# Fetching rounded weights and their remainders with casting and adding DMAs in a two-block transformer kernel

## The chip, the cores and the metric

The kernel runs on one core of a Trainium2 chip. The metric is the time of one execution on the device in microseconds (us), the median of several runs. Below, PE is TensorE, ACT is ScalarE, DVE is VectorE, POOL is GpSimd and SP is SyncE; SP only issues DMAs here. A stall is time in which PE has nothing to do.

## What is computed

Two transformer blocks follow one another on a sequence of 512 tokens with a model width of 1024, all in float32. Cut to the matrix products, which are nearly all of the work:

```python
h = rmsnorm(x, norm_mix_g);  z = h @ w_in                      # 1024 x 5888: q, k, v, gates
y_a, y_b = mixer_a(...) @ w_out_a, mixer_b(...) @ w_out_b      # 1024 x 1024, 256 x 1024
x = x + (gate_a * y_a + gate_b * y_b) @ w_out
x = x + square(relu(rmsnorm(x) @ w_ff1)) @ w_ff2               # hidden 4096
x = x + sigmoid(rmsnorm(x) @ w_ple_gate) * (p @ w_ple)         # 1024 x 1024, 256 x 1024
...
x = x + 0.5 * (silu(h @ ffn1_w1) * (h @ ffn1_w3)) @ ffn1_w2    # second block, hidden 2816
x = x + hybrid_mixer(rms_norm(x), w_in_2, ...)                 # 1024 x 3584
x = x + memory_attention(rms_norm(x), rms_norm(mem), ...)      # mem: 256 rows; w_kv 1024 x 2048
x = x + 0.5 * (silu(h @ ffn2_w1) * (h @ ffn2_w3)) @ ffn2_w2
return rms_norm(x, norm_out)
```

## The kernel before

Every product is made of three, since TensorE is fed rounded numbers (type float32r, "fp32r" in the rows): a number a is split into its rounded value a_h and the remainder a_l = a - a_h, and w x = w_h x_h + w_h x_l + w_l x_h. Activations are kept transposed, features on the 128 partitions and the 512 tokens beside them, as pairs of tiles `h_h` and `h_l`. The weights are used once each. They lie in HBM in the order of use, cut into **panels** of 128 rows by 1024 columns (512 KB): the 8 blocks of 128x128 that make 128 output features out of 1024 inputs. A panel is 8 x 3 matmuls of 512 columns. Some panels are short: those of `w_out_b` and `w_ple` have 2 blocks (128x256, 128 KB, 6 matmuls) and alternate with full ones, of `w_out_a` and of `w_ple_gate`. Those for the 256 rows of `mem` are full panels whose matmuls have 256 columns. Let i be the number of a panel.

A panel passes through three buffers, chosen by i mod 3. SP loads it into `raw` (`load_panel`, L2728 to L2733). ACT copies each half of it, 128x512, into `wh`, which rounds it (`prep` of `scalar`, which records its copy at L1749). DVE, or POOL for a few panels, subtracts: `wl` = `raw` - `wh` (`prep` of `vector`, L2114, and of `gpsimd`, L2681). PE takes `wh` and `wl` (`mm_k`, L1459). A `raw` buffer is free for the next load once its subtraction is done; `wh` and `wl` are free once PE has used the panel (the event `("used", i)`, a PE signal). Panels 0 and 1 come in three pieces each (`load_piece`, `piece`), so that PE can start early.

The order of each engine's instructions is fixed when the kernel is built. `put` appends a step to `plan` and gives it a time on each engine from the guesses in `LENGTHS`; ACT, DVE and POOL then run their steps in the order of these times, SP in the order of `plan`. Each engine runs strictly in its order and waits where it stands. In `run`, when PE starts panel i, the load of panel i + 3 and the preparation of panel i + 2 are planned:

```python
            if part == 0:
                put("load", p.i + 3)
                put("prep", p.i + 2, 0)
            began[0] = clock[PE] - .5
            if part == parts // 2:
                put("prep", p.i + 2, 1)
```

Beside this, ACT and DVE move results out of PSUM, split activations, do the norms and the softmax. POOL adds the squares for the norms (`norm_add`, L2689, tile `ssum`) and multiplies in the SwiGLU (`silu`, L2693). In the step `ple`, which follows each `w_ple_gate` panel, two norms are summed at once, so that POOL has two adds for each pair of panels. Early in the kernel SP also writes a table of position biases to HBM (`d_tab`), waits until it has landed, and reads it back in twelve DMAs (`spread_table`); the weight loads planned after it stand behind it in SP's queue.

Of the kernel before, what the change touches and what calls it, by code (L numbers as in the profile page):

```python
# [187 lines left out]
def panel_banks(p, *args):  # L188
# [42 lines left out]
    "row1": ((ACT, .6), (DVE, .7)), "piece": ((ACT, .4), (DVE, .45)), "prep": ((ACT, .61), (DVE, .7)), "square": ((ACT, .6),), "add": ((POOL, 1.4),), "mean": ((ACT, .6), (DVE, .7)),  # L231
# [37 lines left out]
class Panel:  # L269
    def __init__(self, i, off, spec, ops, use, n, first, blocks, low):  # L270
        self.i, self.off, self.spec, self.ops, self.use, self.n, self.first = i, off, spec, ops, use, n, first
        self.blocks, self.low, self.ncol = blocks, low, len(spec[3])
        self.width = spec[2] * self.ncol
        if i < 2:
            self.cuts = [slice(0, 256), slice(256, 512), slice(512, 1024)]
        else:
            self.cuts = [slice(o, min(o + 512, self.width)) for o in range(0, self.width, 512)]
        self.done, self.landed = ("used", i), ("raw", i)
# [5 lines left out]
def build(nc, d):  # L284
# [23 lines left out]
    raw_t = [at(f"raw{i}", [128, 1024], O_RAW + 4 * i) for i in range(3)]  # L308
    wh_t = [at(f"wh{i}", [128, 1024], O_W + 8 * i, F32R) for i in range(3)]
    wl_t = [at(f"wl{i}", [128, 1024], O_W + 8 * i + 4, F32R) for i in range(3)]  # L310
# [425 lines left out]
    put("load", 2)  # L736
    put("load_mats")
    put("load_table")
    for i in (3, 4):
        put("load", i)  # L740
# [6 lines left out]
    for k in range(KT):  # L747
        clock[PE] = max(clock[PE], placed["row1", k]) + 1.36
        put("mm1", k)
        if k == 3:  # L750
            put("prep", 2, 0)
    put("prep", 2, 1)
    put("prep", 3, 0)
    put("prep", 3, 1)
# [634 lines left out]
    def last_halves(w2, ks, acts):  # L1389
# [16 lines left out]
        for h in range(2):  # L1406
            for n, p in enumerate(ps):
# [4 lines left out]
                if not h:  # L1412
                    put("prep", p.i + 2, 0)
                    put("prep", p.i + 2, 1)
# [17 lines left out]
    landed = [Signal(f"landed{i}", 16) for i in range(3)]  # L1432
# [15 lines left out]
    def tensor(e, gate):  # L1448
# [30 lines left out]
        def mm_k(p, k, n=slice(0, 512), use=None, last=False):  # L1479
            t, c, use = p.ops[k], p.piece(k), use or p.use  # L1480
            out = use.ap[:, 0:n.stop - n.start]
            wh, wl = (w[p.i % 3][:, 128 * k:128 * k + 128] for w in (wh_t, wl_t))
# [11 lines left out]
        def mm_blocks(p, i):  # L1494
# [3 lines left out]
            for k in range(nk):  # L1498
                t, c, b = p.ops[p.spec[1][0] + k], p.piece(k), p.blocks[i]
                wh, wl = (w[p.i % 3][:, 256 * k:256 * k + 256] for w in (wh_t, wl_t))  # L1500
# [238 lines left out]
    def scalar(e, gate):  # L1739
# [32 lines left out]
        def prep(i, c):  # L1772
            if i >= len(panels) or c >= len(panels[i].cuts):
                return
            p = panels[i]
            gate.wait_ge(p.landed, ("used", i - 3) if i > 2 else None)
            copy(wh_t[i % 3][:, p.cuts[c]], raw_t[i % 3][:, p.cuts[c]]).then_inc(*rounded.mark(("hi", i, c)))
# [312 lines left out]
        steps = {"start": start, "piece": piece, "prep": prep, "row1": row1, "square": norm_square, "mat_r": round_mats,  # L2090
# [17 lines left out]
    def vector(e, gate):  # L2108
# [20 lines left out]

        def prep(i, c):  # L2130
            if i >= len(panels) or c >= len(panels[i].cuts) or panels[i].low != "vector":
                return
            cut = panels[i].cuts[c]
            gate.wait_ge(("hi", i, c))
            sub(wl_t[i % 3][:, cut], raw_t[i % 3][:, cut], wh_t[i % 3][:, cut]).then_inc(*rest_left.mark(("lo", i, c)))
# [516 lines left out]
        steps = {"start": start, "piece": piece, "prep": prep, "row1": row1, "add": norm_add, "mean": mean, "rms": rms,  # L2652
# [21 lines left out]
    def gpsimd(e, gate):  # L2674

        def prep(i, c):
            if i >= len(panels) or c >= len(panels[i].cuts) or panels[i].low != "gpsimd":
                return
            cut = panels[i].cuts[c]
            gate.wait_ge(("hi", i, c))  # L2680
            e.tensor_tensor(wl_t[i % 3][:, cut], raw_t[i % 3][:, cut], wh_t[i % 3][:, cut].bitcast(F32), ALU.subtract).then_inc(*rest_left_g.mark(("lo", i, c)))  # L2681
# [19 lines left out]
        steps = {"prep": prep, "add": norm_add, "silu": silu, "last_out": last_out}  # L2701
# [6 lines left out]
    def sync(e, gate):  # L2708
# [17 lines left out]

        def load_panel(i):
            if i >= len(panels):  # L2728
                return
            p = panels[i]  # L2730
# [46 lines left out]
        steps = {"start": start, "load_x": load_x, "load_piece": load_piece, "load": load_panel, "load_mats": load_mats,  # L2777
# [68 lines left out]
```

## Time and profile before

| | |
|---|---|
| median of 3 runs | 2086.63 us (2085.16 to 2087.03) |
| the profiled execution's own time | 2087.62 us |
| its span, first to last instruction | 2085.8 us |
| mean granted TensorE clock, share of full speed | 0.985 |
| PE busy | 2041.7 us, 98% |
| DVE, ACT, POOL busy | 1212.0, 907.2, 220.7 us |
| moved by DMA | 191.53 MB, mean 92 GB/s |

PE busy is near the span. The difference, 44.1 us, is the idle time of PE. The granted clock tells at which of its two levels, 2.4 GHz (1.0) and 1.2 GHz, PE ran; a mean between them is a mixture. Durations of single matmuls overlap, so the rate is read from the number of matmuls in a window.

### The profile page before, as it was taken

How to read it: one execution, taken by the hardware profiler on the slowest of the kernel's cores; microseconds unless marked ns; L12 is line 12 of the kernel's file. 1: busy time of each engine (PE TensorE's matmuls, PEld its weight loads, DVE VectorE, ACT ScalarE, POOL GpSimd, SP SyncE). 2: the span in 40 equal slices, each digit the busy share in tenths (PEclk: the TensorE clock that was granted, in tenths of full speed). 3: DMA queues.
4: the chain of work that ended last, by engine and by line, in shares of the span. 5: the costliest groups of instructions: out<-in, count | busy, mean ns of one | idle time of the engine just before them, and what ended most of it. 6: DMA issues, size and time to landing. Idle time of an engine off the chain costs nothing.

```text
span 2085.8 us, 24995 instructions
## 1 busy us (share of the span) xinstructions
PE 2041.7 (98%) x9832; PEld 1694.1 (81%) x9832; DVE 1212.0 (58%) x2027; ACT 907.2 (43%) x1749; POOL 220.7 (11%) x170
## 2 busy tenths in 40 slices
PE   8999999999999999999999999999899999999997
PEld 6788888888888888878888888877888788888886
DVE  5768876466444445775544455877776555453444
ACT  4455554345423233643322334766654443332324
POOL 1102220001000001221100011100001011110101
PEclk9999999999999999999999999999999999999998
DMA  4312111243333232323232323222332033333222
GB/s 142 122 62 65 58 61 46 84 155 111 97 96 101 92 101 77 105 81 111 91 101 92 101 90 102 72 86 93 105 112 86 19 109 101 96 97 101 91 91 71
DMA packets 61633, 191.53 MB, mean 92 GB/s; under 512 B 6792, under 2 KB 14472, under 8 KB 61516
## 3 DMA queue, kind: packets, MB, share of 16 engines
q1 hardware_dynamic: 61516, 189.93, 28.6%
q8 instruction: 78, 1.28, 0.2%
q14 instruction: 39, 0.32, 0.1%
HBM read 187.69 MB, written 2.21 MB: 91 GB/s over the span
## 4 chain that ended last, share of the span: by engine, by line
PE 89%; DVE 5%; ACT 3%; DMA 1%; issue 1%; SPq 1%; POOL 0%; DVEq 0%; ACTq 0%
PE bank L1459 88%; PE bank L1463 1%; DVE tmp L2111 1%; DVE wl L2114 1%; SPq L2714 0%; DVE ssum L2111 0%; DVE rsq L2118 0%; DMA d_tab<-tab_sb 0%; ACT rsq L1760 0%; DMA x_sb<-d_xT 0%; ACT rsq L1758 0%; ACT tmp L1752 0%; DMA raw<-d_wts 0%; ACT pa L1885 0%; DVE tmp L2120 0%
## 5 line engine op out<-in xcount | busy, mean ns | idle before, releaser
L1749 ACT ACTIVATE wh<-raw 128x512 fp32r<-128x512 f32 (+1 forms) x698 | 416.6, 611 | 843.0 <-PE bank L1459 815.6
L1459 PE MATMUL bank<-h_h,wh 128*128 128x512 f32 x1536 | 616.4, 401 | 7.3 <-ACT h_h L1749 3.9
L1459 PE MATMUL bank<-h_l,wh 128*128 128x512 f32 x1536 | 601.4, 392 | 1.4 <-DVE h_l L2139 1.4
L1459 PE MATMUL bank<-h_h,wl 128*128 128x512 f32 x1536 | 601.4, 392 | 0.6 <-POOL wl L2681 0.6
L2114 DVE TENSOR_TENSOR wl<-raw,wh 128x512 fp32r<-128x512 f32 (+1 forms) x642 | 485.9, 768 | 90.7 <-ACT wh L1749 82.8
L1459 PEld LDWEIGHTS bank<-h_h,wh 128*128 128x128 f32 x1536 | 290.6, 189 | 72.9 <-ACT wh L1749 5.1
L1459 PEld LDWEIGHTS bank<-h_l,wh 128*128 128x128 f32 x1536 | 290.6, 189 | 62.5 <-issue 3.1
L1459 PEld LDWEIGHTS bank<-h_h,wl 128*128 128x128 f32 x1536 | 289.9, 189 | 62.8 <-POOL wl L2681 1.1
L2111 DVE TENSOR_TENSOR tmp<-bank,rstd 128x512 f32<-128x512 f32 x98 | 70.4, 719 | 119.3 <-PE bank L1459 119.3
L2681 POOL TENSOR_TENSOR wl<-raw,wh 128x512 fp32r<-128x512 f32 x56 | 78.5, 1409 | 333.5 <-ACT wh L1749 333.5
L2111 DVE TENSOR_TENSOR x_sb<-x_sb,bank 128x512 f32<-128x512 f32 (+1 forms) x66 | 42.0, 646 | 122.2 <-PE bank L1459 121.8
L2693 POOL TENSOR_TENSOR tmp<-tmp,rstd 128x512 f32<-128x512 f32 x44 | 59.9, 1362 | 494.6 <-ACT tmp L1920 494.6
L2689 POOL TENSOR_TENSOR ssum<-tmp,tmp 128x512 f32<-128x512 f32 (+1 forms) x9 | 11.8, 1319 | 869.6 <-ACT tmp L1752 869.6
L2395 DVE SCALAR_TENSOR_TENSOR x_sb<-bank,x_sb 128x512 f32<-128x512 f32 x45 | 31.1, 692 | 123.0 <-PE bank L1459 123.0
L1459 PE MATMUL bank<-f1act_h,wh 128*128 128x512 f32 x256 | 99.6, 389 | 0.0
L1459 PE MATMUL bank<-f1act_l,wh 128*128 128x512 f32 x256 | 99.6, 389 | 0.0
L1459 PE MATMUL bank<-f1act_h,wl 128*128 128x512 f32 x256 | 99.6, 389 | 0.0
L2111 DVE TENSOR_TENSOR tmp<-tmp,bank 128x512 f32<-128x512 f32 x53 | 36.3, 685 | 86.5 <-PE bank L1459 83.6
L2689 POOL TENSOR_TENSOR ssum<-ssum,tmp 128x512 f32<-128x512 f32 (+1 forms) x51 | 65.9, 1297 | 146.8 <-ACT tmp L1752 146.6
L1459 PE MATMUL bank<-f3act_h,wh 128*128 128x512 f32 (+1 forms) x194 | 71.8, 370 | 0.0
L1459 PE MATMUL bank<-f3act_h,wl 128*128 128x512 f32 (+1 forms) x194 | 71.7, 369 | 0.0
L1459 PE MATMUL bank<-f3act_l,wh 128*128 128x512 f32 (+1 forms) x194 | 71.6, 369 | 0.0
(485 smaller groups left out, 3296.3 us busy)
## 6 DMA issues: line engine op xcount, KB each, us to landing
raw<-d_wts SPq DMA_DIRECT2D x316, 512.0 KB, 3.5
raw<-d_wts SPq DMA_DIRECT2D x20, 384.0 KB, 3.0
x_sb<-d_xT SPq DMA_DIRECT2D x16, 256.0 KB, 5.0
raw<-d_wts SPq DMA_DIRECT2D x24, 128.0 KB, 2.0
d_yT<-x_sb SPq DMA_DIRECT2D x4, 384.0 KB, 2.9
tab<-d_ali SPq DMA_DIRECT2D x4, 256.0 KB, 3.9
tab<-d_dec SPq DMA_DIRECT2D x4, 256.0 KB, 3.2
mraw<-d_memT SPq DMA_DIRECT2D x8, 128.0 KB, 2.5
```

Source lines behind the costliest of these rows:

```text
L1459: return e.matmul(out, lhsT, rhs, start=opens(use), stop=True, skip_group_check=True)
L1463: return e.transpose(out, in_, ident)
L1749: return e.activation(out, in_, FN.Copy, **kw)
L2111: return e.tensor_tensor(out, a, b, op)
L2114: return e.tensor_tensor(out, a, h.bitcast(F32), ALU.subtract)
L2395: ins = e.scalar_tensor_tensor(x[nb], p.use.ap[:, :], scale, x[nb], ALU.mult, ALU.add)
L2681: e.tensor_tensor(wl_t[i % 3][:, cut], raw_t[i % 3][:, cut], wh_t[i % 3][:, cut].bitcast(F32), ALU.subtract).then_inc(*rest_left_g.mark((" ...
L2689: e.tensor_tensor(s, first, t, ALU.add).then_inc(*summed.mark((norm.key, "sum", k), norm.ts[k].free, norm.ts[0].free if k == 1 else None))
L2693: e.tensor_tensor(t.ap[:, :], t.ap[:, :], norm.r.ap[:, :], ALU.mult).then_inc(*summed.mark(("silu_r", p.i)))
```

## The change

The weights no longer pass through `raw` (except panels 0 and 1, which are loaded as before). POOL issues for each panel a DMA from HBM straight into `wh`; its destination has the type float32r, so the transfer converts. ACT then writes `wl` = -`wh` in one instruction of 128x1024. POOL issues a second DMA which reads the same weights from HBM again and adds them to `wl` in SBUF: `wl` = -`wh` + weights. DVE's and POOL's subtractions are gone. The space of the `raw` buffers makes a fourth pair `wh`, `wl` (on the place of the two `raw` buffers of panels 0 and 1). Buffers go by i mod 4, and the load of panel i + 3, planned at the start of panel i, waits until PE has used panel i - 1. SP keeps only the other loads and the output.

```diff
             if part == 0:
                 put("load", p.i + 3)
-                put("prep", p.i + 2, 0)
-            began[0] = clock[PE] - .5
-            if part == parts // 2:
-                put("prep", p.i + 2, 1)
+                put("rest", p.i + 2)
...
     def scalar
-        def prep(i, c):
-            gate.wait_ge(p.landed, ("used", i - 3) if i > 2 else None)
-            copy(wh_t[i % 3][:, p.cuts[c]], raw_t[i % 3][:, p.cuts[c]]).then_inc(*rounded.mark(("hi", i, c)))
+        def rest(i):
+            if i < len(panels):
+                gate.wait_ge(("hi", i, 0))
+                copy(wl_t[i % 4][:, 0:panels[i].width], wh_t[i % 4][:, 0:panels[i].width].bitcast(F32), scale=-1.0).then_inc(*rounded.mark(("minus", i)))
...
     def gpsimd
-        def prep(i, c):
-            gate.wait_ge(("hi", i, c))
-            e.tensor_tensor(wl_t[i % 3][:, cut], raw_t[i % 3][:, cut], wh_t[i % 3][:, cut].bitcast(F32), ALU.subtract).then_inc(...)
+        def load_panel(i):
+            if i < len(panels):
+                p = panels[i]
+                gate.wait_ge(*[("used", i - 4)] if i > 3 else [("lo", n, 2) for n in range(2)] if i == 3 else [])
+                e.dma_start(wh_t[i % 4][:, 0:p.width], source(p)).then_inc(*landed[i % 4].mark(("hi", i, 0)))
+
+        def rest(i):
+            if i < len(panels):
+                p = panels[i]
+                gate.wait_ge(("minus", i))
+                e.dma_start(wl_t[i % 4][:, 0:p.width], source(p), accum_op=ALU.add).then_inc(*added[i % 4].mark(("lo", i, 0)))
...
     def sync
-        def load_panel(i):
-            if i > 2:
-                gate.wait_ge(("lo", i - 3, len(panels[i - 3].cuts) - 1))
-            e.dma_start(raw_t[i % 3][:, 0:p.width], source(p)).then_inc(*landed[i % 3].mark(p.landed))
```

The order of SP's queue around `spread_table`, before. `raw_49` to `raw_51` are the three `raw` buffers, `bias` the bias tiles:

```order
L2733 DMA raw_51<-d_wts 128x1024 [waits s_rest_left_g]
L2733 DMA raw_49<-d_wts 128x1024 [waits s_rest_left]
L2714 DMA d_tab<-tab_sb 32x1x893 [waits s_dve_computed]
L2714 DMA bias_85<-d_tab 128x1x256 [waits s_loaded_row]
L2714 DMA bias_85<-d_tab 128x1x256 x3
L2714 DMA bias_86<-d_tab 128x1x128 x4
L2714 DMA bias_87<-d_tab 128x1x128 x4
L2714 DMA sel_sb<-d_sel 128x1028
L2714 DMA rope_sb<-d_rope 128x1024
L2733 DMA raw_50<-d_wts 128x1024 [waits s_rest_left_g]
```

and in the changed kernel:

```order
L2707 DMA mats_sb<-d_mats 128x648
L2707 DMA relb_sb<-d_relb 32x12
L2707 DMA hot_sb<-d_hot 32x893
L2707 DMA mask_sb<-d_mask 4x893
L2707 DMA d_tab<-tab_sb 32x1x893 [waits s_dve_computed]
L2707 DMA bias_86<-d_tab 128x1x256 [waits s_loaded_row]
```

No weight load stands behind the bias table any more; the weight loads are on POOL. POOL's queue of the changed kernel in the pairs of `w_ple` (128x256) and `w_ple_gate` (128x1024), one pair and the start of the next; `wh_51` to `wh_54` are the four `wh` buffers and `wl_55` to `wl_58` the `wl` beside them, `ssum_71` and `ssum_72` the sums of the two norms:

```order
L2682 TENSOR_TENSOR ssum_72<-ssum_72,tmp_64 128x512 [waits s_pool_computed,s_act_computed]
L2682 TENSOR_TENSOR ssum_71<-ssum_71,tmp_60 128x512 [waits s_pool_computed,s_act_computed]
L2668 DMA wh_52<-d_wts 128x1024 [waits s_banked]
L2668 DMA wh_53<-d_wts 128x256 [waits s_banked]
L2674 DMA wl_55<-d_wts 128x256 [waits s_rounded]
L2674 DMA wl_56<-d_wts 128x1024 [waits s_rounded]
L2682 TENSOR_TENSOR ssum_72<-ssum_72,tmp_62 128x512 [waits s_pool_computed,s_act_computed]
```

Before, POOL's queue had only the adds here:

```order
L2689 TENSOR_TENSOR ssum_71<-ssum_71,tmp_62 128x512 [waits s_pool_computed,s_act_computed]
L2689 TENSOR_TENSOR ssum_70<-ssum_70,tmp_59 128x512 [waits s_pool_computed,s_act_computed]
L2689 TENSOR_TENSOR ssum_71<-ssum_71,tmp_61 128x512 [waits s_pool_computed,s_act_computed]
```

Now two adds, which wait for ACT's squares, stand ahead of two loads and two adding DMAs in each pair. In the pairs of `w_out_b` and `w_out_a` POOL has in both kernels no adds, and now these rows:

```order
L2668 DMA wh_54<-d_wts 128x1024 [waits s_banked]
L2674 DMA wl_57<-d_wts 128x256 [waits s_rounded]
L2668 DMA wh_51<-d_wts 128x256 [waits s_banked]
L2674 DMA wl_58<-d_wts 128x1024 [waits s_rounded]
L2668 DMA wh_52<-d_wts 128x1024 [waits s_banked]
```

The load of a panel waits for PE (`s_banked`), the adding DMA for ACT (`s_rounded`).

## Rows read from the trace of the kernel before

**Rows 1.** The page: busy time; PE's share of the chain that ended last.

```profile
PE 2041.7 (98%) x9832; PEld 1694.1 (81%) x9832; DVE 1212.0 (58%) x2027; ACT 907.2 (43%) x1749; POOL 220.7 (11%) x170
...
PE 89%; DVE 5%; ACT 3%; DMA 1%; issue 1%; SPq 1%; POOL 0%; DVEq 0%; ACTq 0%
```

**Rows 2.** The page: costliest groups, busy and mean ns of one, then idle before.

```profile
L1749 ACT ACTIVATE wh<-raw 128x512 fp32r<-128x512 f32 (+1 forms) x698 | 416.6, 611 | 843.0 <-PE bank L1459 815.6
L2114 DVE TENSOR_TENSOR wl<-raw,wh 128x512 fp32r<-128x512 f32 (+1 forms) x642 | 485.9, 768 | 90.7 <-ACT wh L1749 82.8
L2681 POOL TENSOR_TENSOR wl<-raw,wh 128x512 fp32r<-128x512 f32 x56 | 78.5, 1409 | 333.5 <-ACT wh L1749 333.5
L2693 POOL TENSOR_TENSOR tmp<-tmp,rstd 128x512 f32<-128x512 f32 x44 | 59.9, 1362 | 494.6 <-ACT tmp L1920 494.6
```

**Rows 3.** Windows: PE, PEld, DVE, ACT, POOL busy (count), PEclk, DMA share, GB/s.

```profile
10.00:20.00 10.00, 8.48 (x30) 6.55 (x30) 8.44 (x13) 8.76 (x17) 2.23 (x2) 0.83 0.88 316
55.00:75.00 20.00, 15.19 (x77) 11.39 (x76) 12.87 (x23) 9.77 (x26) 2.97 (x2) 0.83 0.47 170
560.00:800.00 240.00, 240.00 (x1060) 198.74 (x1059) 101.62 (x153) 76.16 (x128) 0.00 (x0) 1.00 0.31 97
885.00:915.00 30.00, 25.65 (x99) 19.80 (x98) 18.52 (x23) 14.55 (x24) 8.46 (x6) 0.89 0.23 70
1450.00:1480.00 30.00, 22.84 (x103) 18.66 (x102) 23.86 (x45) 18.28 (x40) 6.42 (x7) 0.77 0.22 72
1490.00:1530.00 40.00, 40.00 (x306) 38.70 (x306) 33.21 (x70) 26.95 (x59) 0.00 (x0) 1.00 0.47 148
1535.00:1550.00 15.00, 11.97 (x40) 9.11 (x39) 10.19 (x17) 7.09 (x13) 0.00 (x0) 0.77 0.30 105
```

**Rows 4.** Timeline, 37 to 67 us: start, duration, engine, line, [idle before <-releaser].

```profile
37.46 0.77 SPq L2714 DMA_DIRECT2D d_tab<-tab_sb  x1
43.70 7.30 SPq L2714 DMA_DIRECT2D bias<-d_tab  x12
...
52.02 14.11 SPq L2733 DMA_DIRECT2D raw<-d_wts  x5
57.62 0.63 ACT L1749 ACTIVATE wh<-raw 128x512 fp32r<-128x512 f32 x1 [16.02 <-DMA raw<-d_wts]
...
58.31 0.50 PE L1459 MATMUL bank<-h_h,wh 128*128 128x512 f32 x1 [1.55 <-ACT wh L1749]
59.67 0.50 PE L1459 MATMUL bank<-h_h,wl 128*128 128x512 f32 x1 [0.63 <-POOL wl L2681]
66.79 0.96 PE L1463 MATMUL bank<-mats_sb,tmp 128*128 128x128 f32 x4 [2.64 <-DVE tmp L2111]
```

**Rows 5.** The chain that ended last, 885 to 898 us: start, length, what.

```profile
885.19 3.88 DVE wl L2114 x3
...
892.54 3.25 DVE wl L2114 x2
```

**Rows 6.** The page: DMA issues, count, size, median us from issue to landing.

```profile
raw<-d_wts SPq DMA_DIRECT2D x316, 512.0 KB, 3.5
raw<-d_wts SPq DMA_DIRECT2D x20, 384.0 KB, 3.0
...
raw<-d_wts SPq DMA_DIRECT2D x24, 128.0 KB, 2.0
```

**Rows 7.** Timeline, PE at two short panels of `w_ple`; ACT and POOL between and behind.

```profile
841.50 0.39 PE L1459 MATMUL bank<-p_op_h,wh 128*128 128x512 f32 x1
848.30 0.39 PE L1459 MATMUL bank<-p_op_h,wh 128*128 128x512 f32 x1
...
848.56 0.42 ACT L1749 ACTIVATE wh<-raw 128x256 fp32r<-128x256 f32 x1 [1.09 <-PE bank L1459]
...
856.38 2.55 POOL L2689 TENSOR_TENSOR ssum<-tmp,tmp 128x512 f32<-128x512 f32 x2 [18.54 <-ACT tmp L1752]
```

**Rows 8.** The timeline, 17 to 22 us: POOL and DVE side by side.

```profile
17.77 3.95 POOL L2681 TENSOR_TENSOR wl<-raw,wh 128x512 fp32r<-128x512 f32 x2 [17.33 <-ACT wh L1749]
18.18 4.09 DVE L2111 TENSOR_TENSOR ssum<-ssum,tmp 128x512 f32<-128x512 f32 x3
22.80 0.68 DVE L2111 TENSOR_TENSOR ssum<-ssum,tmp 128x512 f32<-128x512 f32 x1
```

More of the change, by code:

```diff
@@ L230 @@
 LENGTHS = {
-    "row1": ((ACT, .6), (DVE, .7)), "piece": ((ACT, .4), (DVE, .45)), "prep": ((ACT, .61), (DVE, .7)), "square": ((ACT, .6),), "add": ((POOL, 1.4),), "mean": ((ACT, .6), (DVE, .7)),
+    "row1": ((ACT, .6), (DVE, .7)), "piece": ((ACT, .4), (DVE, .45)), "load": ((POOL, 1.),), "rest": ((ACT, 1.02), (POOL, 1.)), "square": ((ACT, .6),), "add": ((POOL, 1.4),), "mean": ((ACT, .6), (DVE, .7)),
     "mean_mm": ((PE, .45),), "rms": ((ACT, 1.9), (DVE, 1.4)), "rcol": ((DVE, 2.8),), "table": ((PE, .5), (DVE, 1.1)),
@@ L276, in __init__ @@
         else:
-            self.cuts = [slice(o, min(o + 512, self.width)) for o in range(0, self.width, 512)]
-        self.done, self.landed = ("used", i), ("raw", i)
+            self.cuts = [slice(0, self.width)]
+        self.done = ("used", i)
     def piece(self, k):
@@ L735, in build @@
     put("load_x", (4, 5, 6, 7))
-    put("load", 2)
     put("load_mats")
     put("load_table")
-    for i in (3, 4):
-        put("load", i)
+    put("load", 2)
     for k in range(KT):
@@ L750, in build @@
         if k == 3:
[L751 to L754, printed above, removed]
+            put("rest", 2)
+            put("load", 3)
+    put("rest", 3)
+    put("load", 4)
     for k in range(KT):
@@ L1412, in last_halves @@
                 if not h:
-                    put("prep", p.i + 2, 0)
-                    put("prep", p.i + 2, 1)
+                    put("rest", p.i + 2)
                 if h and not n:
@@ L1428, in build @@
         clock[PE] += .1
-    landed = [Signal(f"landed{i}", 16) for i in range(3)]
+    landed, added = ([Signal(f"{n}{i}", 16) for i in range(4)] for n in ("landed", "added"))
     pieces = [[Signal(f"piece{i}_{c}", 16) for c in range(3)] for i in range(2)]
@@ L2088, in spread @@
             return bass.AP(ap.tensor, a[:, 128 * i:128 * i + 1].offset, [list(ap.ap)[0], [384, i + 1], [1, 128]])
-        steps = {"start": start, "piece": piece, "prep": prep, "row1": row1, "square": norm_square, "mat_r": round_mats,
+        steps = {"start": start, "piece": piece, "rest": rest, "row1": row1, "square": norm_square, "mat_r": round_mats,
                  "mean": mean, "rms": rms, "qkb_lo": local_qk_lo, "vb_lo": local_v, "bs_exp": local_exp, "lse": lse,
@@ L2650, in spread @@
             return bass.AP(ap.tensor, a[:, 128 * i:128 * i + 1].offset, [list(ap.ap)[0], [384, i + 1], [1, 128]])
-        steps = {"start": start, "piece": piece, "prep": prep, "row1": row1, "add": norm_add, "mean": mean, "rms": rms,
+        steps = {"start": start, "piece": piece, "row1": row1, "add": norm_add, "mean": mean, "rms": rms,
                  "rcol": rcolumns, "table": table, "qkb": local_qk, "qkb_lo": local_qk_lo, "vb": local_v, "vb_lo": local_v_lo,
@@ L2674, in gpsimd, with source @@
     def gpsimd(e, gate):
[L2676 to L2681, printed above, removed]
+        def source(p):
+            return d["wts"][p.off:p.off + 128 * p.width].rearrange("(p n) -> p n", p=128)
+        def load_panel(i):
[8 more added lines that the diff above has]
+                e.dma_start(wl_t[i % 4][:, 0:p.width], source(p), accum_op=ALU.add).then_inc(*added[i % 4].mark(("lo", i, 0)))
         def norm_add(norm, k):
@@ L2699, in last_out @@
                 e.tensor_tensor(xs[:, k, HALF[h]], xs[:, k, HALF[h]], last_use[0].ap[:, HALF[h]], ALU.mult).then_inc(*summed.mark(("y", k, h)))
-        steps = {"prep": prep, "add": norm_add, "silu": silu, "last_out": last_out}
+        steps = {"load": load_panel, "rest": rest, "add": norm_add, "silu": silu, "last_out": last_out}
         for _, _, name, args in sorted(orders[POOL - 1], key=lambda entry: entry[:2]):
```

22 lines of the change are left out of this document (6 added, 16 removed).

## The prediction

> **What bounds the kernel now.** The page comes first: PE is busy 2041.7 of 2085.8 us, and 89% of the chain that ended last is PE's own work [rows 1]. So a faster preparation of weights can give back only the 44.1 us in which PE stands, and what the clock loses round these places. The windows show where they are [rows 3]. In the long middle of a feed-forward part PE has no gap and a full clock: 1060 matmuls in 240 us, 0.226 us each, so a panel of 24 takes 5.43 us. Around 55 to 75, 885 to 915, 1450 to 1480 and 1535 to 1550 us PE is idle 4.8, 4.35, 7.2 and 3.0 us, and the clock is at 0.83, 0.89, 0.77 and 0.77, which is 3.4, 3.3, 6.9 and 3.4 us more. The waits, the timeline and the chain of each such place say who is late. The same windows show the DMA engines: 0.31 busy at 97 GB/s in the feed-forward part, and 316 GB/s at 0.88 where they are pressed, so 359 GB/s when full. At that rate a panel's 512 KB take 1.46 us.
>
> **What the change takes away.** 642 subtractions on DVE (485.9 us) and 56 on POOL (78.5 us) go, and 698 ACT copies of 0.61 us become some 358 of about 1.0 us, 0.61 plus twice the 0.2 us by which 128x512 exceeds 128x256 [rows 2, 7]. All of it lies beside PE almost everywhere, so it is worth only what it does at the four places.
>
> - 55 to 75 us. SP writes the bias table at 37.46, waits for it, reads it back in twelve DMAs until 51.0, and only then, at 52.02, issues weight loads. ACT waits 16.0 us for one of them, and in its strict order the activations stand behind it: PE waits 1.55, 0.63 and 2.64 us [rows 4]. Now the loads are on POOL and do not stand behind the table. I take the whole: 4.8 + 3.4 = 8.2 us. Low end 4, since table, bias and rope tiles now share the DMA engines with twice as many weight transfers.
> - 885 to 915 us. On the chain, DVE subtracts for weights 3.88 and 3.25 us ahead of the residual that PE waits for [rows 5]. They go. Of 4.35 + 3.3 I take 7 us; low end 3, if the same rows then wait for ACT.
> - 1450 to 1480 us. Here it is mostly a chain of small activations; DVE is busy 23.9 of 30 us [rows 3]. I take 3 of 14 us; ends 0 and 8.
> - 1535 to 1550 us. An activation chain as well; I take 1.5 us; ends 0 and 4.
> - The start. POOL's two subtractions and DVE's adds hold each other up there: three adds take 4.09 us where one alone takes 0.68, and POOL's two take 3.95 for 2 x 1.41 [rows 8, 2]. That goes, some 2 us. Against it, panel 2's DMA waits for nothing now, and its 1.46 us get between the first pieces and x. I set the two against each other: 0, ends -3 and +4.
>
> Sum of gains: 8.2 + 7 + 3 + 1.5 = 19.7 us.
>
> **What it adds.** No row shows a converting or an adding DMA, or any DMA issued by POOL. The nearest are SP's plain loads, 3.5 us from issue to landing for 512 KB [rows 6], and POOL's own instructions of 1.4 us [rows 2]. For POOL to issue one I take 0.7 us more than SP needs (ends 0 and 1.4). A converting DMA I take at the price of a plain one, 1.46 us of the engines (ends 1 and 2 times that), so it lands 3.5 + 0.7 = 4.2 us after POOL comes to it. The adding one must read 512 KB twice, HBM and its own destination; I take 2 times (ends 1 and 3), and a landing after 3.5 + 0.7 + 1.5 = 5.7 us.
>
> Collectives: The Full Stack, of the Trainium skill, says in Part 3 that an add in the DMA path needs two source reads and thereby halves the rate (32 against 62 GB/s); no run here shows it yet. DMA: Bandwidth & Descriptors, of the same skill, gives 2.0 us plus bytes/436 GB/s for a DMA from POOL (Anatomy of one DMA), 3.2 us for a panel by that; the sum would lose about 1 us per pair below.
>
> Three places then. **Full panels**: engine time (1 + 2) x 1.46 = 4.4 us of 5.43. It fits. The chain from "used i - 1" to panel i + 3 is 4.2 + 1.0 + 5.7 = 10.9 us, and there are 3 panels, 16.3 us. Hidden. The cover is gone above 3.7 times the plain price for both DMAs together.
>
> **Short pairs.** Two short panels lie 6.80 us apart, 1.36 for itself and 5.43 for the full one [rows 7]. A full panel's load waits until the full panel before it is used, and then only a short, a full and a short panel lie ahead: 8.15 us, and 0.45 until the first matmul that takes `wl`, 8.6. The chain is 10.9. If PE loses s per pair, the window grows by 2s: s = (10.9 - 8.6)/2 = 1.15 us, for 8 pairs of `w_out_b` 9 us. In the 8 pairs of `w_ple` two adds stand ahead of the loads in POOL's queue. Before, they end at 858.93, 10.6 us after the gate panel before 848.30 [rows 7]; with a period of 6.8 + s they hold the load up by 3.8 - s. So 14.7 - s = 8.6 + 2s: s = 2.0, 16 us. Here ACT's order adds to it: its `rest` waits for a landing, with squares and sigmoids behind it, on which DVE and POOL wait.
>
> **The panels of mem**, 1490 to 1530 us: 148 GB/s for 40 us is 5.9 MB, 16.5 us at full rate, 49 us at three times. Nine too many; the panels ahead on chip cover about 4. I take 5 us; ends 0 and 25.
>
> Sum: -19.7 + 9 + 16 + 5 = +10.3 us. The profiled execution's own time is 2087.6, which gives 2098; the median is 1 us lower, so **2097 us**.
>
> **The rivals.**
>
> 1. *Slightly slower, as summed.* Chance 0.31; its own range is 2091 to 2140.
> 2. *Faster.* The gains stay and the short pairs have no wait. It takes one mechanism: the adding DMA lands like a plain one and POOL's issue costs no more than SP's: 3.5 + 1.0 + 3.5 = 8.0, below the 8.6 us of the window [rows 6]. It decides at 8.6. Left are about 6 us from the adds and 5 of mem: -19.7 + 11 = -9, 2078 us; 2066 if those go too. For it speaks that the DMA share is only 0.31; against it that a second read is never free. Chance 0.27.
> 3. *No change*, gains and new waits within 4 us of each other, or both small because the stalls are activation chains: 2087. Chance 0.12.
> 4. *The DMA engines become the bound.* Above 3.7 times the plain price each panel costs more than 5.43 us: at 4 times (each DMA twice) 5.84, at 4.5 times 6.57. Over the 336 large panels [rows 6] that is +135 and +380 us: 2220 to 2470; each DMA three times, 8.8 us, would be beyond 3100. For it speaks that 3 times already fills 0.81 of the engines; against it the rate of 359 GB/s, far above the 290 that would be needed. Chance 0.2.
> 5. *POOL becomes the bound.* Two DMAs per panel, and half a multiplication of 1.36 us in the SwiGLU: if issuing takes over (5.43 - 0.68)/2 = 2.4 us each, POOL sets the pace; at 3 us it is +0.6 to +1.2 us a panel, 2290 to 2490. For it: POOL's and DVE's instructions held each other up, 4.09 us for 2.04 of work [rows 8, 2], and writing a DMA's description may meet the same. SBUF — State Buffer, of the Trainium skill, states this as a rule (the "DVE blocks DMA" trap, for DVE copies in a two-port mode); rows 8 show only adds and subtractions. Against it: nothing on POOL took over 2 us. Chance 0.1.
>
> **How the numbers follow.** Two kernels within 0.2%, 4.2 us, can't be told apart. Faster is rival 2, 0.27; same is rival 3, 0.12; slower are 1, 4 and 5, 0.61. The range goes from 2066, the low end of rival 2, to 2480, nearly the upper ends of 4 and 5. Outside are some 0.06 below and 0.12 above.
>
> **What would show it.** In the profile after: no PE wait near 58 us and no DVE work for weights near 885 us shows the gains; PE waits on `wl` by DMA once per pair near 370 to 440 and 835 to 890 us show the short pairs; DMA share about 0.8 and 1060 matmuls in 240 us in the feed-forward part show that the engines keep up. A share near 1 there with fewer matmuls is rival 4. A POOL queue issuing back to back, with the engines idle between, is rival 5. I would be wrong above all in the price of the adding DMA: it is taken from plain loads alone.

## The result and the profile after

The changed kernel takes 2147.48 us in the median (2144.89 to 2151.0, 4 runs) against 2086.83 for the kernel before (4 runs): 1.0294 times, 95% interval 1.0282 to 1.0307. It is slower, as forecast, but by 60.7 us where 10 were forecast. The time lies beyond rival 1's own end of 2140 and far below rival 4's 2220.

The page of the changed kernel: busy time, the queue that carries the weights, the costliest groups on ACT and POOL, and the DMA issues with their median time to landing.

```profile
PE 2051.9 (95%) x9832; PEld 1693.6 (79%) x9832; DVE 737.3 (34%) x1391; ACT 856.0 (40%) x1413; POOL 645.4 (30%) x826
...
q0 software_dynamic: 102528, 352.37, 76.1%
...
L1743 ACT ACTIVATE wl<-wh 128x1024 fp32r<-128x1024 f32 (+2 forms) x356 | 356.9, 1003 | 364.7 <-DMA wh<-d_wts 364.6
...
L2668 POOL DMA_DIRECT2D wh<-d_wts x356 | 204.4, 576 | 892.8 <-PE bank L1453 884.5
L2674 POOL DMA_DIRECT2D wl<-d_wts x356 | 311.7, 877 | 513.0 <-ACT wl L1743 509.7
...
wh<-d_wts POOLq DMA_DIRECT2D x316, 512.0 KB, 4.4
wl<-d_wts POOLq DMA_DIRECT2D x316, 512.0 KB, 5.6
```

DVE lost 475 us of work and PE gained nothing by it. PE is idle 2149.4 - 2051.9 = 97.5 us, where it was 44.1 [rows 1]: 53.4 more. It is also busy 10.2 us longer. Together that is the 63.6 us by which the span grew. The prices were nearly as forecast: 4.4 us to land for the converting DMA (4.2 in the sum), 5.6 for the adding one (5.7), 1.0 us for the negative. POOL issues a DMA in 0.6 to 0.9 us, so rival 5 did not come.

PE's waits in the changed kernel, the longest two groups (us in total, times, the longest):

```profile
PE bank L1453 <- DMA wl<-d_wts: 64.0, 39, 5.1
PE bank L1457 <- DVE tmp L2103: 5.1, 1, 5.1
```

The new wait, 64.0 us, is more than the whole new idle time; all other waits together shrank by 10.6 us. The same view by stretch places the wait on `wl`: 13.6 us from 360 to 530 (the `w_out_b` pairs), 15.0 from 840 to 985 (`w_ple`), 15.4 from 1480 to 1600 (the panels of mem), 12.5 from 1700 to 1810 (`mem_w_o`, where four panels of 128x256 stand in a row ahead of full ones). That is 56.5 of the 64.0. At the pairs themselves it is 8.8 us (400 to 455) and 10.5 us (850 to 920); the rest of the first two stretches falls on full panels just ahead of them and behind them.

Windows of the changed kernel (columns as in [rows 3]):

```profile
55.00:75.00 20.00, 14.86 (x86) 11.72 (x85) 8.26 (x17) 6.43 (x19) 3.71 (x5) 0.91 0.76 187
560.00:800.00 240.00, 240.00 (x1060) 198.79 (x1060) 46.54 (x68) 74.28 (x91) 63.15 (x89) 1.00 0.90 194
885.00:915.00 30.00, 24.77 (x100) 19.36 (x99) 8.47 (x12) 12.24 (x20) 19.28 (x21) 0.94 0.75 154
1500.00:1540.00 40.00, 31.43 (x213) 29.03 (x212) 22.51 (x51) 24.86 (x49) 9.43 (x13) 0.91 0.82 178
1550.00:1580.00 30.00, 23.32 (x160) 22.30 (x159) 5.70 (x14) 11.41 (x20) 8.55 (x12) 0.89 0.96 219
1735.00:1765.00 30.00, 23.01 (x83) 18.12 (x82) 8.30 (x8) 8.60 (x12) 11.89 (x13) 0.83 0.64 137
```

In the feed-forward part 1060 matmuls still fit into 240 us, at a DMA share of 0.90: the engines keep up and rival 4 did not come. In the panels of mem they are nearly full, 0.96 from 1550 to 1580 us. A window at a place of waits shows why PE's busy time grew as well: from 1735 to 1765 us the granted clock is 0.83, and 83 matmuls keep PE busy for 23.01 us, 0.277 each against 0.226.

The chain that ended last, at a pair of `w_out_b` and `w_out_a` (start, length, what):

```profile
399.96 6.13 PE bank L1453 x27
406.10 0.35 issue
406.44 4.07 DMA wh<-d_wts
...
410.54 1.07 ACT wl L1743
411.61 0.42 issue
412.03 5.55 DMA wl<-d_wts
417.58 0.04 issue
417.62 6.92 PE bank L1453 x22
```

From PE's release of the buffer at 406.10 to the arrival of `wl` at 417.62 it is 11.5 us; my sum had 10.9. The two `issue` pieces of 0.35 and 0.42 us, which I had left out, make the difference.

Not every wait on `wl` is this chain alone. In 7 of the 39, 12.4 us in all, ACT came to the negative only 2 us or more after `wh` had landed, since other steps stood ahead of it; in 5, 8.2 us in all, POOL issued the adding DMA more than 1 us after the negative, since the load of a later panel stood ahead of it and waited for PE. Both can be seen in the timelines of ACT and POOL from 1738 to 1765 us:

```profile
1738.21 1.04 ACT L1743 ACTIVATE wl<-wh 128x1024 fp32r<-128x1024 f32 x1
1748.62 0.55 POOL L2668 DMA_DIRECT2D wh<-d_wts  x1 [9.57 <-PE bank L1453]
1749.19 0.90 POOL L2674 DMA_DIRECT2D wl<-d_wts  x1
...
1763.60 0.72 ACT L1743 ACTIVATE h_h<-x_sb,cols_sb 128x512 fp32r<-128x512 f32 x1 [7.94 <-DVE x_sb L2103]
1764.22 1.05 ACT L1743 ACTIVATE wl<-wh 128x1024 fp32r<-128x1024 f32 x1
```

The negative is written at 1739.25, but its adding DMA is issued at 1749.19, behind a load that PE released; PE then waits 1.9 us. The negative at 1764.22 is for a panel whose load was issued at 1748.62 and landed at 1753.0; it stood behind `h_h`, for which ACT waited 7.9 us, and cost PE 2.4 us.

### The profile page after: what moved, and what is told of

Read it like the earlier page. It is cut to its first block, busy times and chain, and to the rows that moved or that the text cites. A ratio compares the mean times of both kernels' runs of the same rounds, so it can differ in the third digit from the quotient of the medians.

```text
span 2149.4 us, 23983 instructions
## 1 busy us (share of the span) xinstructions
PE 2051.9 (95%) x9832; PEld 1693.6 (79%) x9832; DVE 737.3 (34%) x1391; ACT 856.0 (40%) x1413; POOL 645.4 (30%) x826
## 4 chain that ended last, share of the span: by engine, by line
PE 80%; DMA 10%; DVE 3%; ACT 3%; issue 2%; POOL 1%; SPq 1%; DVEq 0%; POOLq 0%; ACTq 0%
PE bank L1453 79%; DMA wl<-d_wts 6%; DMA wh<-d_wts 3%; PE bank L1457 1%; DVE tmp L2103 1%; ACT wl L1743 1%; SPq L2707 1%; DMA bias<-d_tab 1%; DMA d_tab<-tab_sb 0%; DVE x_sb L2103 0%; ACT tmp L1746 0%; POOL wl L2674 0%; ACT rsq L1754 0%; POOL wh L2668 0%; DVE rsq L2110 0%
## 5 line engine op out<-in xcount | busy, mean ns | idle before, releaser
L1743 ACT ACTIVATE wl<-wh 128x1024 fp32r<-128x1024 f32 (+2 forms) x356 | 356.9, 1003 | 364.7 <-DMA wh<-d_wts 364.6
L2668 POOL DMA_DIRECT2D wh<-d_wts x356 | 204.4, 576 | 892.8 <-PE bank L1453 884.5
L2674 POOL DMA_DIRECT2D wl<-d_wts x356 | 311.7, 877 | 513.0 <-ACT wl L1743 509.7
L1912 ACT ACTIVATE tmp<-tmp 128x512 f32<-128x512 f32 x44 | 27.8, 632 | 151.9 <-DVE tmp L2103 151.9
L1746 ACT ACTIVATE tmp<-tmp 128x512 f32<-128x512 f32 x58 | 36.5, 629 | 111.9 <-DVE tmp L2390 99.0
```

What stands on the lines that cost most here:

```text
L1743: return e.activation(out, in_, FN.Copy, **kw)
L1746: return e.activation(out, in_, FN.Square, **kw)
L1912: e.activation(t.ap[:, :], t.ap[:, :], FN.Silu).then_inc(*computed.mark(("silu", p.i)))
L2668: e.dma_start(wh_t[i % 4][:, 0:p.width], source(p)).then_inc(*landed[i % 4].mark(("hi", i, 0)))
L2674: e.dma_start(wl_t[i % 4][:, 0:p.width], source(p), accum_op=ALU.add).then_inc(*added[i % 4].mark(("lo", i, 0)))
```

## The experiments

Kernels named below that keep the chain and the adding DMA have the changed kernel's code but for the edit shown. `before` was run beside each group; its medians were 2086.14 (bench to adds_dve), 2087.27 (pool_loads to hi_pool), 2087.12 (short_slots2 to in_place_act), 2086.89 (short_slots3) and 2087.51 us (the last two).

**bench.** The DMAs by themselves, four buffers of each kind; nothing of the reference is computed.

```python
e.dma_start(hi[b][:, :], src(n))                        # converting
e.dma_start(lo[b][:, :], src(n), accum_op=ALU.add)      # adding
```

> No part of the reference is computed: this kernel only moves panels of 128x1024 from HBM to SBUF, first one at a time (four of each kind), then with four buffers in flight (sixteen of each): plain from SP, converting from POOL, adding from POOL, and last converting and adding in turn, as the changed kernel has them. If the read of the own destination is the price (my step: converting 1, adding 2 times plain), the streams run at about 1.5 us a panel plain and converting, 3 us adding, 4.4 us for a pair. If converting and adding are both slow in themselves, the pair takes above 5.4 us and the DMA engines were the bound. Alone, one at a time, I expect 3.5, 4.2 and 4.7 to 5.7 us.

POOL's timeline, each DMA waiting for the one before:

```profile
50.20 0.53 POOL L319 DMA_DIRECT2D hi<-d_wts  x1 [3.08 <-DMA hi<-d_wts]
53.90 0.53 POOL L319 DMA_DIRECT2D hi<-d_wts  x1 [3.18 <-DMA hi<-d_wts]
...
63.33 0.91 POOL L319 DMA_DIRECT2D lo<-d_wts  x1 [4.80 <-DMA lo<-d_wts]
68.77 0.88 POOL L319 DMA_DIRECT2D lo<-d_wts  x1 [4.52 <-DMA lo<-d_wts]
```

Windows with four of a kind in flight: converting, adding, and both in turn (DVE, POOL, PEclk, DMA share, GB/s):

```profile
85.00:103.00 18.00, 0.00 (x0) 5.83 (x11) 1.00 1.07 372
112.00:146.00 34.00, 0.00 (x0) 11.24 (x13) 1.00 1.05 201
165.00:205.00 40.00, 0.00 (x0) 15.70 (x22) 1.00 1.08 277
```

Alone, a converting DMA of 512 KB comes round every 3.7 us and an adding one every 5.4. In flight, 372 GB/s make 1.41 us for a converting one (plain ones ran at 394 GB/s from 22 to 32 us, 1.3 us), 201 GB/s make 2.61 for an adding one, and one of each takes 3.8 at 277 GB/s, of the 5.43 us that a full panel has. So the adding DMA costs 1.9 times a converting one, and the engines are not the bound for full panels. (The bench ran once.) Collectives: The Full Stack, of the Trainium skill (Part 3), says that an add in the path halves the rate by its two source reads; the measured 1.9 agrees.

**no_chain.** The same traffic without the chain. From panel 6 on ACT's negative is left out as well, so the remainders are not computed, and nothing on ACT waits for a landing of weights from there on.

```diff
         def load_panel(i):
             e.dma_start(wh_t[i % 4][:, 0:p.width], source(p)).then_inc(...)
+            if i > 5:
+                e.dma_start(wl_t[i % 4][:, 0:p.width], source(p), accum_op=ALU.add).then_inc(...)
```

> The changed kernel, but from panel 6 on ACT no longer writes the negative, and POOL issues the adding DMA right behind the converting one; it adds the weights to what the buffer held, so the remainders are wrong. The DMA traffic is the same, only the chain load - ACT - second DMA is gone. Theory 1 (the chain of two DMAs in series is longer than the panels ahead last, at the short panels): the 64 us of waits on wl go, time 2075 to 2095. Theory 2 (the DMA engines' throughput): the waits stay, above 2125. Theory 3 (order on POOL: norm adds stand ahead of the loads): the waits in the pairs of w_ple stay, about 15 us, the others go, about 2100.

2082.41 us, 0.9983 times before (0.9973 to 0.9993), 65 us less than the changed kernel at the same 367.6 MB. The wait on `wl`:

```profile
PE bank L1453 <- DMA wl<-d_wts: 11.3, 12, 3.2
```

Each DMA lands later than in the changed kernel (5.5 and 7.6 us against 4.4 and 5.6), the engines' share is higher, and it does not matter, since both are issued three panels ahead. The wait left at the first three places is 0.4, 0.7 and 2.3 us. This kernel reaches `mem_w_o` some 58 us sooner, at 1660 to 1690 us, and has one wait on `wl` there, of 1.7 us, behind one on `wh` of 2.0. So three reads per panel alone do not cost the 65 us: it takes the series of load, negative and adding DMA, together with the places of its steps in ACT's and POOL's strict orders, which went with it here.

**no_add.** The second DMA only converts; the chain stays, the remainder is not formed.

```diff
-                e.dma_start(wl_t[...], source(p), accum_op=ALU.add).then_inc(...)
+                e.dma_start(wl_t[...], source(p)).then_inc(...)
```

> The changed kernel, but the second DMA does not add: it writes the converted weights over the negative, so the remainders are wrong. The chain of three steps stays, the traffic falls from three reads to two per panel. Theory 1: the chain shortens by the difference of the two landings, 1.2 us (5.6 to 4.4), so 64 us of waits fall to about 40, time about 2120. Theory 2: the engines are relieved by a third, nearly all waits go, below 2095.

2090.75 us, 1.0021 times before (1.0012 to 1.0031); waits on `wl` of 23.1 us. By its time this is the outcome named for theory 2, throughput, not the 2120 us of theory 1. But the relief of the engines also shortens the chain, and by more than the 1.2 us expected: the DMAs land after 3.9 and 4.2 us, 1.9 us less together. no_chain had already shown that the full traffic alone does not cost the time, so theory 2 by itself is out; how the gain divides between fewer bytes and a shorter chain this run cannot tell. The first three places have 4.4, 5.5 and 3.9 us, and `mem_w_o`, here from 1660 to 1720 us, has 6.2. ACT's and POOL's orders are those of the changed kernel. Of the 65 us, 57 go with the last 1.9 us of the chain and with the smaller engine time (5.1 us of them are the wait for the bias table, below): a chain near its window is a cliff.

**adds_dve.** The norms' adds on DVE (`who="vector"`), so that POOL's queue has none between the DMAs.

> The changed kernel with the adds of the norms on DVE and not on POOL. Theory 3 (adds that wait for squares hold up the loads behind them in POOL's queue): the waits in the pairs of w_ple and near 1730 to 1770 us fall by half or more, 15 us faster, about 2132. Theory 1 alone: within 5 us of the changed kernel, since the window of 8.6 us against a chain of 11 us stays.

2147.41 us, as the changed kernel; 63.0 us of waits on `wl`, 13.7 of them from 840 to 985 us, against 15.0. The adds ahead of the loads cost next to nothing: my reason for the larger loss at `w_ple` was wrong.

**pool_loads.** One part of the change alone, on the kernel before: `load_panel` in POOL's program instead of SP's.

```diff
     def gpsimd
+        def load_panel(i):
+            gate.wait_ge(("lo", i - 3, len(panels[i - 3].cuts) - 1))
+            e.dma_start(raw_t[i % 3][:, 0:p.width], src).then_inc(*landed[i % 3].mark(p.landed))
```

> One part of the change alone: the kernel before, with its plain weight loads issued by POOL instead of SP, so that they no longer stand behind the bias table in SP's queue. Rounding, subtraction and three buffers stay. It prices the largest gain that was forecast, 8.2 us at 55 to 75 us, where nothing else presses on the DMA engines. Theory A (the gain exists and the changed kernel loses it again because its DMA traffic delays the bias tiles): 2076 to 2081 us, and the PE waits near 58, 60 and 64 us gone. Theory B (the queue order was not the cause of the stall, an activation chain is): 2085 to 2088 us, the waits moved to other releasers. Each load costs a little more to issue from POOL, hidden either way.

2080.21 us, 0.9967 times before (0.9955 to 0.9978): 7.1 us faster, of the 8.2 that I had for 55 to 75 us. It is faster than both kernels, and PE's waits from 50 to 80 us are 1.2 us, against 4.7 before. SP's timeline round the bias table, in this kernel:

```profile
36.88 0.78 SPq L2723 DMA_DIRECT2D d_tab<-tab_sb  x1
43.16 7.45 SPq L2723 DMA_DIRECT2D bias<-d_tab  x12
```

and in the changed kernel, with DVE's first use of the table:

```profile
29.93 0.78 SPq L2707 DMA_DIRECT2D d_tab<-tab_sb  x1
37.10 16.52 SPq L2707 DMA_DIRECT2D bias<-d_tab  x12
...
63.33 0.69 DVE L2103 TENSOR_TENSOR pB<-bank,bias 128x512 f32<-128x512 f32 x1 [8.85 <-DMA bias<-d_tab]
```

The same twelve issues take 16.52 us there instead of 7.45, and the last of them lands 11.97 us after its issue at 51.27 instead of 6.46. The window from 36 to 52 us has a DMA share of 0.99 in the changed kernel and 0.49 in this one. So the gain is real, and the doubled traffic at the start takes it back: table and bias come too late instead of the loads. In no_add, which has the engines nearly as busy there (0.93 from 34 to 45 us) but moves 253 GB/s against 224, the issues take 10.42 us, and PE has no wait between 50 and 80 us.

**hi_dma, hi_pool.** Only the first half of the change, on the kernel before: `wh` by a converting DMA, three buffers, `raw` loaded by SP (hi_dma) or POOL (hi_pool), DVE subtracts.

```diff
     def gpsimd
+        def load_hi(i):
+            gate.wait_ge(("used", i - 3) if i > 2 else None)
+            e.dma_start(wh_t[i % 3][:, 0:p.width], src).then_inc(*converted[i % 3].mark(...))
     def scalar
-        def prep(i, c): ...
```

> Only the first half of the change, on the kernel before: wh comes by a converting DMA from POOL, raw is still loaded by SP, and DVE (or POOL) still subtracts. ACT's rounding copies are gone, there is no adding DMA and no second DMA behind an ACT step. HBM traffic is the same as in the changed kernel, engine time 2 instead of about 2.9 units per panel. From the issue to wl it is then 4.2 + 0.8 us instead of 11.5, against windows of 7 us and more with three buffers. Lookahead theory: no wl waits at the short panels, 2080 to 2090 us; below 2086 if ACT's 417 us of copies also stood in front of activations at the stalls of 885 and 1450 us. Throughput theory: between 2100 and 2140.

> The same as the version with only wh by a converting DMA, and the plain loads of raw also issued by POOL, ahead of it. If both gains exist (no loads behind the bias table, no rounding copies on ACT) they add up: 2074 to 2080 us. If POOL's queue, in which two DMAs, the adds and some subtractions now stand, holds loads up, it is above the better of the two single versions.

2175.61 us (1.0435, 1.0406 to 1.0463) and 2186.3 us (1.0461, 1.0438 to 1.0484): both expectations failed, and these are the slowest of all, though they have neither adding DMA nor long chain. The page of hi_dma:

```profile
L2111 DVE TENSOR_TENSOR wl<-raw,wh 128x512 fp32r<-128x512 f32 (+1 forms) x642 | 436.9, 696 | 885.5 <-DMA wh<-d_wts 881.4
```

Its waits of PE:

```profile
PE bank L1463 <- ACT rsqr L1753: 13.9, 3, 6.4
PE bank L1463 <- DVE vml L2571: 8.3, 1, 8.3
PE bank L1463 <- DVE tmp L2108: 7.7, 3, 3.0
PE bank L1463 <- DVE mem_hl L2550: 7.2, 5, 2.5
```

DVE stood 881 us before subtractions, waiting for a DMA that was released only when PE had used the buffer, and in its strict order the activations stood behind. Before, the same subtraction waited for ACT's copy of 0.6 us, 83 us in all [rows 2]. Of PE's waits, 104 us in all, some 12 are for weights, the others for activations. That this order is the cause is read from these waits; in_place, below, where DVE's waits for landings fall to 72 us, agrees, but it changes the buffers too.

**short_slots, short_slots2, short_slots3.** The short panels of `w_out_b` and `w_ple` in two buffers of their own, in three orders.

```diff
+    wh_t += [at(f"wsh{i}", [128, 256], O_G + 2 * i, F32R) for i in range(2)]
+    wl_t += [at(f"wsl{i}", [128, 256], O_G + 2 * i + 1, F32R) for i in range(2)]
+    buf = {i: 4 + n % 2 for n, i in enumerate(short)}
+    buf.update((i, n % 4) for n, i in enumerate(full))
```

> The changed kernel with a ring of two own small buffers for the 16 short panels of w_out_b and w_ple, in space that is free at that time; the four large buffers then hold only full panels there. All DMAs, ACT steps and the traffic are the same. Lookahead theory: a full panel is then loaded three full panels ahead there too, so the PE waits on wl between 360 and 520 us (13.6 us) and between 840 and 970 us (15.0 us) go but for 2 or 3 us, and the rest stays: 2147 less 25 to 32 us (each wait also costs 0.27 us in the matmul behind it), 2115 to 2122 us. Throughput theory: the same bytes in the same time, 2140 to 2148 us. Theory of a slow mixing of the two blocks (the activation chains of the pairs are late, the waits on wl only stand in front of them): the wl waits go and DVE or ACT waits take their place, 2135 to 2147 us.

> The version with two own small buffers for the short panels, with one thing changed: the negative and the adding DMA of a short panel are issued one panel later, so that they find it landed. In the run before, the chain showed POOL's strict order as a loop of 7.9 us per pair: load of a short panel, 5.5 us until it lands, ACT's negative, the adding DMA, and only behind it the next load. If that loop was what was left of the waits at the pairs, they go now from 360 to 450 and 845 to 975 us (19.9 us): 2138 less about 25, 2110 to 2117 us. If the waits at the pairs are a matter of throughput or of the other chains, 2133 to 2140 us.

> The same as the version before with own buffers for the short panels, with one more thing changed: between short panels the negative and the adding DMA of a full panel are no longer planned two panels ahead but as soon as its load has had two panels of time, three full panels ahead of its use. In the two earlier versions the buffers were early but this step stayed tied to the count of two panels, so the window from the negative to the first use stayed 8.6 us while the adding DMA took 7.9 us behind a load just issued. If the lookahead is what counts, the waits of PE on wl of full panels in 360 to 450 and 845 to 975 us (8.3 us) go, those on the short ones (14.2 us) shrink: 2120 to 2135 us. If they stay, what binds in the pairs is POOL's strict order or the DMA engines, not the number of panels ahead: 2140 to 2150 us.

2138.28, 2150.65 and 2142.95 us (1.0251, 1.0309, 1.0272, each within 0.003): that gives back 9, -3 and 4 us, where 25 to 32, 30 to 37 and 12 to 27 were expected; the third lies in the range named for POOL's strict order or the DMA engines as the bound. The chain of short_slots in the pairs shows what took over:

```profile
405.82 7.91 DMA wsh<-d_wts
413.73 0.02 issue
413.75 0.43 ACT wsl L1758
414.18 0.42 issue
414.60 0.88 POOL wsl L2695
415.47 0.05 issue
415.53 0.56 POOL wl L2695
416.09 5.32 DMA wsh<-d_wts
```

PE is not in it. A short panel's load must land, ACT negates, POOL issues the adding DMAs, and only then POOL comes to the next short load: 7.7 to 8.1 us round, against 6.80 for a pair. In the other two orders PE stands in the chain again, but a short panel's adding DMA, 128 KB, takes 5.4 and 5.5 us in the median, where it took 3.1 in short_slots, and its planned place is one panel ahead. So more buffers alone did not lengthen the lookahead; that the strict queues and the plan's step count hold it is what the chains show, no run frees them.

**nc_short, nc_full.** In the changed kernel the chain is taken from one kind of panel in the pairs only, as in no_chain; these panels' negative is left out.

```diff
+                if p.spec[0] in ("w_out_b", "w_ple"):        # nc_full: ("w_out_a", "w_ple_gate")
+                    e.dma_start(wl_t[i % 4][:, 0:p.width], source(p), accum_op=ALU.add).then_inc(...)
```

> The changed kernel, in which only the 16 short panels (w_out_b and w_ple) have their adding DMA issued right behind their converting one; ACT's negative of these 16 is left out, so their remainder is not computed. The full panels keep the chain, the traffic is the same. If the chain of the short panels themselves (load, negative, adding DMA in the strict orders of ACT and POOL) is what binds in the pairs: the waits on wl from 360 to 530 and 840 to 985 us (28.5 us) go but for a few, 2115 to 2122 us. If it is the chain of the full panels, with only 8.6 us ahead of them: little changes, 2138 to 2148 us.

> The counterpart: only the full panels that alternate with short ones (w_out_a and w_ple_gate, 16) have their adding DMA issued right behind the converting one, without ACT's negative; the short panels and all others keep the chain. If the chain of the full panels binds (my prediction's place, 10.9 us against 8.6): 28.5 us of waits go, 2115 to 2122 us. If that of the short panels: 2138 to 2148 us. If each takes over when the other is gone, both of these versions stay above 2130 us.

2147.99 and 2142.87 us (1.0305 and 1.0262, each within 0.0031). The waits on `wl` in the two stretches of the pairs, 28.6 us in the changed kernel, are 25.3 and 18.0 us here, and 1.1 us in no_chain. From 400 to 455 and 850 to 920 us, at the pairs alone, they are 19.3 us in the changed kernel, 19.8 and 13.9 here. So the chain of either kind is enough to hold the pairs up; each takes over, wholly or for the most part, when the other is gone. My prediction had only the full panels'.

**in_place, in_place_act.** Two DMAs per panel without a chain: plain into the place of `wl`, converting into `wh`, both when a buffer is free; DVE subtracts in place; four buffers of 8 KB. in_place_act has the plain DMA alone and lets ACT round.

```diff
+                gate.wait_ge(*[("used", i - 4)] ...)
+                e.dma_start(plain_t[i % 4][:, 0:p.width], src).then_inc(...)
+                e.dma_start(wh_t[i % 4][:, 0:p.width], src).then_inc(...)     # not in in_place_act
```

> A version without the chain that keeps the two DMAs per panel: both are issued together by POOL when a buffer is free, a converting one into wh and a plain one into the place of wl, where DVE (or POOL) subtracts wh in place. So a panel needs 8 KB of a partition, and four fit, as in the changed kernel. Nothing is left on ACT for weights; the subtraction of short panels and of those of mem is planned one panel later, so that DVE does not wait for a landing. HBM traffic is that of the changed kernel, engine time 2 units per panel instead of 2.9. In the version with three buffers and wh by a converting DMA (2175 us), DVE waited 881 us for landings with the activations behind them. Theory (a step that waits for a landing in a strictly ordered engine is what costs there): 2070 to 2082 us. If the doubled traffic itself delays bias tiles, x and mem panels: 2085 to 2100 us.

> The same four buffers and order with one plain load per panel from POOL, ACT rounding it into wh and DVE subtracting in place: the kernel before with another buffer and its loads on POOL. Traffic is that of before. It gives the base for the version with two DMAs: 2074 to 2081 us. The difference of the two is what the converting DMA saves (ACT's 417 us of copies, which lie beside PE but for the activation chains) less what the second read costs.

2117.1 us (1.0146, 1.0131 to 1.0161) and 2091.63 us (1.0022, 1.0012 to 1.0031): both miss. In in_place DVE now waits only 72 us for landings. PE's longest waits there:

```profile
PE bank L1465 <- DVE pta_l L2113: 10.4, 3, 3.8
PE bank L1469 <- DVE tmp L2110: 7.8, 1, 7.8
PE bank L1465 <- DVE mem_hl L2555: 4.2, 4, 2.5
PE bank L1465 <- DVE qa2l L2113: 3.6, 1, 3.6
```

The 7.8 us are the bias table's place again: DVE waits 8.1 us for `bias` there. So two DMAs per panel cost 25 us against in_place_act even without adding DMA and long chain. The second read and DVE's waits for the converting DMA come together in this number; no run parts them. in_place_act differs from pool_loads in buffers and order only and is 11 us slower, which agrees with PE's waits (43.0 against 31.3 us in all), above all one of 5.4 us for ACT's `rsqr` early on; what in the order makes it late was not taken apart.

## Why the prediction missed, step by step

- **Prices of the new operations**: right. Landings 4.4 and 5.6 us (4.2 and 5.7), the adding DMA 1.9 times a converting one (2), the chain 11.5 us (10.9).
- **Full panels hidden**: right. No wait on `wl` from 530 to 840 us, 1060 matmuls in 240 us.
- **The chain without the queues**: the sum let the adding DMA go as soon as ACT was done. But the orders of ACT and POOL are strict, and a third of the waits on `wl`, 20.6 of 64.0 us, has a step that came late in one of them (above). One form is POOL's: the adding DMA of panel i + 2 can stand behind the load of panel i + 3, which waits for PE to use panel i - 1; then only two panels lie ahead of it, not three. So the negative that ends at 363.8 us has its adding DMA issued at 367.5, right behind such a load; it lands after 8.2 us, and PE waits 1.3 us for it.
- **Pairs, 9 + 16 us**: the mechanism is shown, since no_chain leaves 1.1 us. The stretches have 13.6 and 15.0 us of waits, the pairs themselves 8.8 and 10.5. So 9 was met and 16 was too much: what made it 16 and not 9 was POOL's adds, and adds_dve refutes them. That the sum of both is near the two stretches is partly luck, for 9.3 us lie outside the pairs. The short panels also have a chain of their own that binds (nc_full).
- **The panels of mem, 5 us**: mis-sized; 15.4 us. I asked there only whether the engines can move the bytes, and forgot the chain. Their matmuls start every 0.12 us in the kernel before, so a panel takes 2.9 us, and three ahead with the start of the fourth are 8.9 us. By the formula of the pairs, a loss s per panel widens the window by 3s: (11.5 - 8.9)/3 = 0.87, and 16 panels of `w_kv` give 14 us. That is an estimate, and it takes the landings of a quieter place: with the engines 0.96 busy, the eight adding DMAs that PE waited for here landed after 5.6 to 8.2 us. no_chain supports the chain as the cause, since at equal traffic 2.3 us are left; but its last four waits end 3.7 to 3.8 us apart, the time that the engines need for a panel in the bench, so there the engines' bound is just behind.
- **`mem_w_o`, nothing**: 12.5 us, a place that is missing in the sum. [rows 6] shows 24 loads of 128 KB; 4 belong to panels 0 and 1 and 16 to the pairs, and I did not ask for the other four. They stand in a row, so that only three of them and half a microsecond, some 4.5 us, lie ahead of the first full panel. PE waits 8.3 us in three steps up to that panel; the other 4.3 us are the two late steps shown above, of POOL and of ACT. no_add has 6.2 us here, and no_chain 1.7 us with 2.0 for `wh`.
- **Elsewhere, nothing**: 7.5 us of waits on `wl` lie outside the four places, 3.0 of them before 50 us and 2.6 behind 2120 us.
- **The gains, 19.7 us**: about half came. All waits but those on `wl` shrank by 10.6 us. At 55 to 75 us the gain is real by itself (7.1 us in pool_loads), but it was taken back by the bias table's late landing, 5.1 us of wait; my low end of 4 had that mechanism but not its size. At 885 us DVE's subtractions went, and PE's wait of 3.9 us for `h_h` with them, but waits on `wl` stand in its place; no_chain shows the gain free, 0.7 us of waits from 840 to 985 us against 4.3. The chain of activations near 1450 us is hardly changed: its waits for `mem_hl` come later in the changed kernel, and no_chain has 5.8 us there against 6.9.
- **What a wait costs**: I priced the new waits by idle time alone. PE is 10.2 us longer busy than before, and 16.3 us longer than in no_chain (2051.9 against 2035.6), with the same number of matmuls; the windows place it where the clock falls.

In sum, the step that failed is the list and the size of the new waits: the chain was asked for at the pairs only, 30 us with mem's bytes, and the waits on `wl` are 64.0. The gains were 10.6 us of idle time where 19.7 were forecast with the clock's share, and 10.2 us of busy time for the new waits were not in the sum: 64.0 - 10.6 + 10.2 = 63.6, the growth of the span.

Still open is how to keep the pairs free of waits with this scheme: buffers alone did not do it, and the plan's order was tried in three forms only.

## What to carry to other kernels

When work moves from an engine to a DMA, compare the whole chain from the buffer's release to the last landing with the time of the panels ahead, at every place where panels are short or quick, and list those places from the rows rather than from memory. Count in what stands ahead of each step in its engine's order. Once a chain exceeds its window the loss comes back at each panel: here 1.9 us of chain, with the lighter traffic that went with them, were worth 57 us. Do not let a strictly ordered engine wait for a transfer that has only just been released (881 us of DVE's idle time in hi_dma), and try the parts of such a change alone: moving the loads to POOL's queue was the one that paid.

## What was not expected of the hardware

- Twelve small DMAs of the bias table took 7.5 us to issue from SP at a DMA share of 0.49 (pool_loads) and 16.5 us at 0.99 (changed kernel), so busy DMA engines go with slower issue even on another queue. The share alone does not set it: in no_add, without adding DMAs, it was 10.4 us at 0.93.
- A converting DMA costs hardly more than a plain one in flight (1.4 against 1.3 us per 512 KB). Alone it landed 3.4 us after its issue, and the next one could be issued after 3.7. DMA: Bandwidth & Descriptors, of the Trainium skill (Anatomy of one DMA), gives 3.2 us by its formula; that is near the 3.4 us alone, and beside the other traffic of the kernel it was 4.4.
- A DMA of 128 KB took 3.3 us (converting) and 3.5 us (adding) in the median of the changed kernel, but the adding one 5.5 us in short_slots3, issued close behind full panels, where a full panel's took 5.6: its size hardly counted then.
